# A two-block transformer kernel: each head's output-norm step placed ahead of the next head's scores and softmax

## The reference

```python
# first block: two layers, 16 heads each (dilated, neighbourhood, memory attention), residual; not touched
# second block, x of 256 x 2048:
h = rms_norm_2(x, norm1_w); z = h @ w_in
y_ssm  = s5_mixer(z[..., :1024], ...)                    # state-space mixer, gelu, GLU
y_attn = diff_attention(q, k, v of z, ...)               # 8 heads, below
m = sigmoid(z_gs) * (y_ssm @ w_proj_ssm) + sigmoid(z_ga) * (y_attn @ w_proj_attn)
x = x + m @ w_out;  x = x + ffn(rms_norm_2(x, norm2_w))

def diff_attention(...):                                  # per head: q, k of 2 maps x 64 wide, v of 128
    q, k = rms_norm_2(q) * 64 ** -0.5, rms_norm_2(k)
    s = q k^T + bias[rel. position]                       # two score maps of 256 x 256, block-causal mask
    p = softmax(s);  p = p[map 0] - lam * p[map 1]
    o = p @ v                                             # 256 x 128
    return rms_norm_2(o, subln_w, 1e-5) * (1 - lambda_init)   # the output norm, per head
```

## Time and profile before

| | |
|---|---|
| median of 3 executions | 2533.4 us (2530.65 to 2544.58) |
| the profiled execution | 2544.58 us, of which the span in the trace is 2542.9 us |
| PE matmuls busy | 2468.0 us, 97% |
| PE weight loads busy | 2344.0 us, 92% |
| DVE busy | 1695.1 us, 67% |
| ACT busy | 1220.5 us, 48% |
| POOL busy | 640.5 us, 25% |
| rounds 1 to 9 of the weave | about 1130 to 1395 us of the span |

### The profile page before, as it was taken

The page is one execution under the profiler, slowest core; times in us unless marked ns, Lnnn a source line. Parts: engine busy times, 40 slices in busy tenths (PEclk is TensorE's granted clock), DMA queues, the critical chain, the costliest instruction groups (busy, mean ns, idle before and its releaser), DMA issues.

```text
span 2542.9 us, 50531 instructions
## 1 busy us (share of the span) xinstructions
PE 2468.0 (97%) x18072; PEld 2344.0 (92%) x18072; DVE 1695.1 (67%) x2556; ACT 1220.5 (48%) x1814; POOL 640.5 (25%) x1047
## 2 busy tenths in 40 slices
PE   7899999999999999999998999999999999999999
PEld 7899999889999998999998899999888888888888
DVE  7877676558887777678887665665555555555555
ACT  5445444455566655555664334434444444444442
POOL 3310032149899995210011221001000000000000
PEclk9999999999999999999999899999999999999999
DMA  6665566555655555546555676665766766777764
GB/s 231 202 197 190 182 211 201 163 189 178 196 193 194 195 187 165 183 165 200 161 186 181 219 234 222 196 206 183 193 187 187 186 188 187 187 187 185 188 183 157
DMA packets 217449, 484.85 MB, mean 191 GB/s; under 512 B 22760, under 2 KB 120724, under 8 KB 217088
## 3 DMA queue, kind: packets, MB, share of 16 engines
q1 hardware_dynamic: 182912, 415.29, 54.0%
q0 software_dynamic: 13216, 37.93, 4.8%
q10 hardware_dynamic: 21216, 30.22, 3.6%
HBM read 455.00 MB, written 31.08 MB: 191 GB/s over the span
## 4 chain that ended last, share of the span: by engine, by line
PE 81%; DVE 10%; issue 4%; ACT 3%; DMA 1%; ACTq 1%; DVEq 0%
PE z_ps L2002 16%; PE z_ps L2003 15%; PE z_ps L2004 15%; PE z_ps L2338 6%; PE z_ps L2339 6%; PE z_ps L2344 6%; DVE w_lo L1299 4%; ACT w_hi L717 1%; PE o_ps L2041 1%; PE s_ps L2023 1%; PE o_ps L2373 1%; PE o_ps L2372 1%; PE o_ps L2371 1%; PE v_ps L2373 1%; PE v_ps L2372 1%
## 5 line engine op out<-in xcount | busy, mean ns | idle before, releaser
L2002 PE MATMUL z_ps<-x_hi,w_hi 128*128 128x256 f32 x2816 | 820.7, 291 | 17.3 <-DVE w_lo L1292 14.3
L1299 DVE TENSOR_TENSOR w_lo<-w_raw,w_hi 128x1024 fp32r<-128x1024 f32 x520 | 638.7, 1252 | 286.6 <-ACT w_hi L717 284.1
L2003 PE MATMUL z_ps<-x_lo,w_hi 128*128 128x256 f32 x2816 | 803.4, 285 | 0.0
L2004 PE MATMUL z_ps<-x_hi,w_lo 128*128 128x256 f32 x2816 | 803.1, 285 | 0.0
L717 ACT ACTIVATE w_hi<-w_raw 128x1024 fp32r<-128x1024 f32 x520 | 536.1, 1052 | 302.3 <-PE z_ps L2004 256.8
L2002 PEld LDWEIGHTS z_ps<-x_hi,w_hi 128*128 128x128 f32 x2816 | 547.1, 194 | 24.7 <-issue 15.8
L2003 PEld LDWEIGHTS z_ps<-x_lo,w_hi 128*128 128x128 f32 x2816 | 547.4, 194 | 1.2
L2004 PEld LDWEIGHTS z_ps<-x_hi,w_lo 128*128 128x128 f32 x2816 | 546.8, 194 | 0.0
L1892 DVE TENSOR_TENSOR w_lo<-w_raw,w_hi 128x1024 fp32r<-128x1024 f32 x262 | 320.7, 1225 | 314.9 <-ACT w_hi L1143 314.9
L1143 ACT ACTIVATE w_hi<-w_raw 128x1024 fp32r<-128x1024 f32 x262 | 277.7, 1060 | 427.9 <-PE z_ps L2344 273.2
L2338 PE MATMUL z_ps<-w_hi,x_hi 128*128 128x512 f32 x704 | 275.1, 391 | 0.6 <-DVE res L1868 0.6
(11 more groups left out here) (382 smaller groups left out, 4138.9 us busy)
## 6 DMA issues: line engine op xcount, KB each, us to landing
w_raw<-in_w SPq DMA_DIRECT2D x704, 512.0 KB, 4.3
w_raw<-in_w SPq DMA_DIRECT2D x80, 384.0 KB, 4.8
res<-tab_d POOLq DMA_DIRECT2D x32, 384.0 KB, 4.5
w_raw<-in_w SPq DMA_DIRECT2D x80, 128.0 KB, 2.8
tab_d<-arena ACTq DMA_DIRECT2D x32, 256.0 KB, 3.9
tab_d<-arena POOLq DMA_DIRECT2D x32, 128.0 KB, 3.0
sg_d<-arena ACTq DMA_DIRECT2D x32, 128.0 KB, 4.6
arena<-sg_d POOLq DMA_DIRECT2D x16, 256.0 KB, 3.8
```

The lines of the kernel that those rows point to most:

```text
L1299: dve.tensor_tensor(w_lo[:, n % RING, :], w_raw[:, n % RING, :], w_hi[:, n % RING, :].bitcast(F32), ALU.subtract).then_inc(w_lo_ready, 1)
L2002: pe.matmul(z, wh, hi[:, kt, :], start=(first and i == 0), stop=False)
L2003: pe.matmul(z, wh, lo[:, kt, :], start=False, stop=False)
L2004: m = pe.matmul(z, wl, hi[:, kt, :], start=False, stop=(last and i == len(kts) - 1))
```

## The change

Three lists are reordered, and nothing is added or taken away in the program's text.

1. PE: `output_sums` stands before `scores2`, in `head_2` and in `gates`.
2. DVE: in `attn_2` the divisor of the output norm (L1618, L1619, L1622) stands before the bias and the maxima. ACT: in `attn_2` the Sqrt stands before the copy and the four Exps.
3. DVE: `attn_3` and `attn_4` become one function `attn_3`. In `head_2` it stands where `attn_4` stood, so the softmax combination (L1629 to L1638) now follows `split_lo(p,4)` and the evacuation of v. In `gates` the two already stood together, and their place there is the same.

```diff
@@ ACT
             def attn_2(i, prev, prev2):
+                if prev2:
+                    act.wait_ge(ov_step, 2 * (i - 1))
+                    act.activation(o_root, ov, ACT.Sqrt).then_inc(o_root_ready, 1)
                 if prev:
                     act.wait_ge(scores2_done, i)
...
                     e.then_inc(exp2_done, 1)
-                if prev2:
-                    act.wait_ge(ov_step, 2 * (i - 1))
-                    act.activation(o_root, ov, ACT.Sqrt).then_inc(o_root_ready, 1)
@@ DVE
             def attn_2(i, prev, prev2):
+                if prev2:
+                    dve.wait_ge(osum_done, i - 1)
+                    dve.tensor_scalar(osq, p_ps[:, 0, :], FLT_MAX * SUB_SCALE ** 2, SUB_SCALE, ALU.is_lt, ALU.mult)
+                    dve.tensor_scalar(ov, p_ps[:, 0, :], 1.0 / P, SUBLN_EPS * SUB_SCALE ** 2,
+                                      ALU.mult, ALU.add).then_inc(ov_step, 1)
+                    dve.wait_ge(ov_step, 2 * (i - 2) + 1)
+                    dve.reciprocal(ov, ov).then_inc(ov_step, 1)
                 if prev:
                     dve.wait_ge(scores2_done, i)
...
                     dve.tensor_reduce(neg_max2[:, 2:4], sc[1], AX_X, ALU.max, negate=True).then_inc(max2_ready, 1)
-                if prev2:
-                    dve.wait_ge(osum_done, i - 1)
...
-                    dve.reciprocal(ov, ov).then_inc(ov_step, 1)
-            def attn_3(i, prev):
+            def attn_3(i, prev, prev2):
...
                     e.then_inc(probs2_ready, 1)
-
-            def attn_4(i, prev2):
                 if prev2:
                     dve.wait_ge(o_root_ready, i - 1)
@@ DVE head_2
                 evac2(qk[:, 1, :], p, 1, 4)
-                attn_3(i, prev)
                 split_lo(p, 4)
                 if prev:
                     dve.wait_ge(scores2_done, i)
                 evac2(v2_t, p, 2, 4)
-                attn_4(i, prev2)
+                attn_3(i, prev, prev2)
@@ PE head_2
                 job2(p, 1, x_hi, x_lo, ring=4)
+                if prev2:
+                    output_sums(i)
                 if prev:
                     scores2(i, prev2)
-                if prev2:
-                    output_sums(i)
                 job2(p, 2, x_hi, x_lo, ring=4)
```

More of the change, by code:

```diff
@@ L1816, in gates @@
                 if attn is not None:
-                    attn_3(*attn[:2])
-                    attn_4(attn[0], attn[2])
+                    attn_3(*attn[:3])
                 section(4 * j + 3)
```

## The result

| | before | changed |
|---|---|---|
| median | 2533.4 us (2530.65 to 2544.58, 5 runs) | 2559.13 us (2557.48 to 2563.05, 5 runs) |
| ratio | | 1.0099, 95% interval 1.0075 to 1.0124 |
| median when both ran again | 2535.83 us (2526.99 to 2545.86, 25 runs) | 2556.54 us (2549.69 to 2563.39, 6 runs) |
| ratio then | | 1.0083, 95% interval 1.0058 to 1.0108 |
| span in the trace | 2542.9 us | 2555.3 us |

The change made the kernel slower, by 0.8 to 1.0%. The forecast was 2554 us in a range of 2541 to 2566. From the two medians of the second row the price is 20.7 us; the sum had said 20.6.

The account below looks back on a forecast made before the run. Matmuls bind almost everywhere, two nearly equal rings of waits the attention rounds. Loop 17.4, round 1 1.0, round 8 0.7 and clock 1.5 make 20.6 us; forecast 2554 us, range 2541 to 2566.

Parts of the forecast that it names:

- What bounds the rounds: Attention rounds: two rings of waits, one through PE, one only DVE and ACT, both 27.6 us; PE has 0.5 us slack.
- The divisor ahead of the maxima: DVE's `attn_2`: maxima end 2.45 us later, so ACT's Exps start at 1233.27 in round 4.
- Sqrt and the added load: ACT's `attn_2`: added 1.28 us table load covered by 0.6 us; upper parts start 0.8 us later.
- The combination: DVE in the loop: probabilities ready at 1241.0, `turn2` 3.2 us later, round 2.9 us longer.
- PE's swap: PE's `output_sums` ahead of `scores2`: costs PE 1.3 us, but not the round, since `turn2` waits until 1241.0 anyway.
- the first rival: Loop: DVE finds room for the late combination, rounds only 1.3 us longer; 2542.5 us, chance 12%.
- Rounds 1 and 8: First loop round 1.0 us later from the moved combination; round 8, in the gates, 0.7 us later.
- The clock: Loop: slow clock after new 1.9 us stalls lengthens `turn2` in half of six rounds, 1.5 us in all.
- Only PE's swap counts: Rival for the loop: late combination finds room on DVE, 7 x 1.3 = 9 us, 2542.5 us; chance 12%.
- The table load is exposed: Rival on ACT: load before the Exps waits for the maxima, 7.7 us more, 2562 us; chance 8%.
- The clock falls in every round: Rival in the loop: slow clock uses up PE's slack, 1.5 us in each of six rounds, 2561 us; chance 12%.
- Sqrt's departure wins: Rival for loop and round 8: Exps keep their place, upper parts come earlier, 4.7 us gained, 2529 us; chance 6%.

Follow-up runs that it names:

- The three single edits: Kernel before with one edit each: PE's two operations swapped, `attn_2` turned over, or combination moved; rounds of 28.70, 29.26 and 29.95 us.
- The run with Sqrt last: Kernel before with DVE's divisor ahead of the maxima, ACT's Sqrt still behind the Exps, no added table load; 2553.21 us, ratio 1.0069.
- the Copy: Changed kernel with the Sqrt of L977 made a Copy, which needs no table; 2552.73 us, ratio 1.0066, rounds of 30.61 us.

## Why the prediction was right

*What bounds the rounds.* Right. Two rings of nearly equal length meet at L954. One passes through PE from `output_sums` to `turn2`, the other only through DVE and ACT. The three single edits show it: each lengthened the round at once.

*The divisor ahead of the maxima.* Right: 2.45 us in the trace after, as taken. The run with Sqrt last shows it without the Sqrt's departure, 30.02 - 27.62 = 2.40 us.

*Sqrt and the added load.* Right. The cover was put at 0.6 us and was 0.46 us; the upper parts came 0.7 us later after `output_sums` (9.48 us for 8.80) for the 0.8 said. The Trainium skill's rule of grouping by table (page "ScalarE: Activation LUTs", section "Table sets: the hidden batching unit") did not decide the time here: the order with the added load was the shorter by 0.76 us a round, because the load lay in a wait. The 2.66 us that the Trainium skill gives for a switch (same page, section "What ACT_TABLE_LOAD costs") would have made the cover negative; in the trace the load took 1.28 us and the Exp still had to wait.

*The combination.* Right in kind and nearly in size: 3.2 us later at `turn2`, less 0.3 at L954, made 2.9. In the trace `turn2` comes 15.40 us after `output_sums` for 12.05, so 3.35 later, and the round is 2.99 us longer. PE's stall there was 1.71 us for the 1.9 said.

*PE's swap.* Right: 1.0 us before `output_sums`, and no price of its own beside the late combination. Alone it is 1.08 us, below the 1.3 us that the first rival used: the prediction took L954's wait of 0.28 us off for the combination and not for the swap.

*Rounds 1 and 8.* Round 1: from one L1578 to the next, rounds 1 and 2 were 28.07 us apart and are now 29.02, 0.95 more for the 1.0 said. Round 8: from L1584 to `turn2` it was 1358.21 - 1330.54 = 27.67 us and is 1373.62 - 1345.3 = 28.3, 0.6 more for 0.7.

*The clock.* This term was wrong. I had put 1.5 us on slow clock after the new stalls of 1.9 us. From 1181 to 1351 us the granted clock was 1.00 in both traces of the changed kernel, and `turn2` took 0.65 us in each of those rounds. What I had not looked for is the slow stretch at `output_sums` of round 2, which lengthened that round in the old kernel's second trace and not in the changed kernel. The sum without the term is 19.1 us, where the weave shows 19.1 and 17.6. That it came to 20.6, and the medians to 20.7, is within the scatter and no merit of the term: by its interval the second ratio allows 15 to 27 us. The fear itself was not empty: with PE's order taken back two stalls were 3 us, and rounds of up to 31.7 us followed.

*The rivals.* "Only PE's swap counts" would have given rounds of 28.9 us and fell with 30.61. Its sum took seven rounds, though by the prediction's own text rounds 1 and 8 pay nothing for the swap: six make 7.8 us, and the swap alone measured 6.9. "The table load is exposed" fell with the Copy. "The clock falls in every round" fell in the changed kernel's own traces. "Sqrt's departure wins" was half right: the departure is worth 0.8 us a round, less than the 2.45 us that the divisor costs.

## What to carry to other kernels

When the engine that is 97% busy has a short stall in every turn of a loop, look at the stall's releaser and follow the ring back to where it closes: here an edit cost what it added to that ring beyond the waits on it, whatever the busy shares of the engines said. Put work that nobody awaits behind work that lets another engine go, and not before it; here that meant combination and upper parts first, divisor and Sqrt later, the opposite of the change. Don't add the prices of single edits: those of three parallel paths came to 5.05 us a round where the whole costs 2.99. And take a second trace of each kernel before reading a price of some us out of a difference of spans: the two spans first read here differ by 12.4 us where the medians differ by 20.7.

## What the runs showed of the hardware

A PE rest in two parts of 1.71 and 1.00 us a round left the granted clock at 1.00 from round 3 to round 7; one rest of 2.99 us was followed by 0.51 from 1248 to 1255 us, around its end. But the length of a rest did not settle what the clock did next. After the same stall of 1.37 us in round 2, `output_sums` took 0.70 us in one execution of the kernel before and 1.11 us in another. With equal stalls of 2.30 and 2.31 us in successive rounds of one kernel, `turn2` once took 0.65 us and once 1.11 us. And `output_sums`, with a stall of 1.46 us in each of two successive rounds of the kernel with only `attn_2` turned over, took 0.70 us once and 1.12 us once:

```profile
1199.29 0.70 PE L2191 MATMUL p_ps<-arena,ones 128*128 128x256 f32 x2 [1.46 <-DVE arena L1604]
...
1228.56 1.12 PE L2191 MATMUL p_ps<-arena,ones 128*128 128x256 f32 x2 [1.46 <-DVE arena L1604]
```

A table load took 1.28 us on ACT in every row read here. Where the instruction that it served had to wait, the load was issued before that wait.
